# A Mamba/HGRN2/PEER block: the first head prepared in the first mixer, a one-hot on another engine, a deeper pipeline in the last head, one gate stage moved, one product for four

## The chip, the cores and the metric

The program runs on one core of a Trainium2 chip. Times are microseconds on the device, from the start of the execution to its end. A time of a kernel is the median of its runs; the profile is one execution more, with its own time.

## What is computed

A block of a sequence model over 1024 tokens of width 1024, all in float32:

```python
hn = rmsnorm(x, ln_mix_w)
z, xbc, dt_raw, q, f, i, g = split(hn @ w_in)
y_ssd = ssd_mixer(z, xbc, dt_raw, ...)      # 16 heads in 4 groups
y_hg = hgrn2_mixer(q, f, i, g, lb, ...)     # 8 heads of 128
h = x + concat(y_ssd, y_hg) @ w_out
h = h + peer_ffn(rmsnorm(h))                # 8 heads, the best 16 of 128 x 128 experts
return rmsnorm(h)
```

In a chunk of the SSD mixer the decays are exp of differences of cumulative sums of `a`; the HGRN2 mixer has the gate `f = lb + (1 - lb) sigmoid(f_raw)`, its logarithm summed within a chunk, and products of q and k weighted by exp of such sums. For each token and head `peer_ffn` takes rows of two tables of 16384 x 1024: `gelu(x . u) * gate * v`, summed.

## The kernel before

It is written by hand for each engine, with semaphores; each engine runs its queue in order. Five blocks follow one another, with a barrier between them: `input_norm`, `ssd`, `hgrn`, `mix_out`, `peer`. A block of tokens ("chunk") has P = 128; there are NB = 8 chunks, in two halves of HC = 4.

`ssd` runs over four groups of four heads. For each chunk TensorE makes a first stage: `ps_cb`, three transposes and `ps_rows`, the cumulative sums spread over rows, as four products with `awide` (GpSimd's `a` times ones) as weights (L424). Behind them it makes two pieces of the next group's projection (`piece`; in the last group `head_piece`, the first HGRN2 head's q, f and v/g pieces, L396 and L399, which ScalarE copies into unused columns of `Y`, L472). Then comes the second stage, `ps_y` and `ps_state` (from L438), for which VectorE must have made `att` (L625); VectorE's state update waits for it (L631). VectorE and ScalarE prepare the next half (`prepare`, four parts, one per chunk, between `att` and the state update). In the last four chunks of the last group there is nothing more to prepare.

`hgrn` starts with a zero fill of the table `sel` in HBM, issued by ScalarE (L857), then copies the pieces from `Y` (L797), and prepares half 0 of head 0 in four parts (`prepare`): sigmoid, affine map, logarithm, a scan, seven levels of differences, exponentials, and products with k and q (the last are L931 and L932). TensorE's first stage of a chunk is L774 to L777 (seven levels, one product k q, a transpose of `ke`), then come pieces of the next head (L755, L759), then the second stage, `ps_state` and two products into `ps_o` (L785 to L788). VectorE masks the levels (L949, L951) and sums them to `att` (L955), prepares a part, and updates the state (L962) and the output (L965). Seven heads run in a loop, the eighth apart: it has no next head's pieces. ScalarE squares its output (L851), and there the rows of `Y` (L845).

`mix_out` is the output projection and the routing of the first four blocks of tokens, whose experts are not gathered but computed densely: a table of gates `sel` says what gate each expert has for each of these tokens. The first block's entries are scattered by GpSimd.

`peer` first makes the entries of `MB` = 3 blocks: 96 groups of four tokens. VectorE compares a row of numbers with the first keys (`hot_a`, one wide compare, L1908) and with the second keys times the gate (`hot_b`, four instructions, L1912), TensorE multiplies them (L1719), ScalarE copies the two halves of the result into stages (`place_out`, L1793 and L1796), two groups in rotation. SyncE stores a stage when 16 groups are in it (L1622); the fourth stage is `ur`, the ring of u rows. At groups 24 and 60 VectorE routes a unit in between. Then SyncE loads the first u columns (L1627), ScalarE loads gates (L1823), and 256 slots run. In each TensorE makes eight products of 128x512 for one expert column (`ps_d`, L1738) or for one output tile (`ps_o`, L1751); VectorE multiplies the hidden values with the gates (L1924), and for the other four blocks makes two dots with gathered u rows (L1937) and adds two gathered v rows (L1948). GpSimd issues the gathers (L1648, L1655), five rows deep in each ring:

```python
pool.wait_ge(sel_out[3], sel_stores(3))
for r in range(RING):
    u_row(r)
for r in range(RING):
    v_row(r)
```

## Time and profile before

| what | us |
|---|---|
| median of three runs (lowest to highest) | 3722.78 (3721.39 to 3723.29) |
| the profiled execution | 3722.1 |
| its span, first to last instruction | 3720.4 |
| TensorE busy | 3466.2 (93%) |
| VectorE busy | 2888.3 (78%) |
| ScalarE busy | 992.5 (27%) |
| GpSimd busy | 1430.4 (38%) |
| end of the first mixer, and of the second | 532.4, 1161.6 |
| start of `peer`, and of its slots | 1610.2, 1810.5 |

A busy share is an average over the five blocks, in which different engines wait; it says nothing of one boundary. So the profile is read in stretches of time: who is idle in one, and what ended the idle time. PE is TensorE, PEld its weight loads, DVE VectorE, ACT ScalarE, POOL GpSimd, SP SyncE; a `q` behind a name is the engine's issuing of DMAs. A 128x512 float32 product appears as two passes.

### The profile page before, as it was taken

The numbers are of one execution on the slowest core, as the hardware profiler recorded it, in microseconds if no ns is written. First come the engines' busy times: TensorE is split into PE (matmuls) and PEld (weight loads), VectorE is DVE, ScalarE is ACT, GpSimd is POOL, SyncE is SP. The second block draws the span as 40 slices with busy tenths as digits, with TensorE's granted clock in tenths as the row PEclk, the third lists the DMA queues.
The fourth block names the chain that finished last, engine by engine and source line by source line (L and its number), as shares of the span: only waits on it lengthen the run. The fifth ranks groups of instructions, "written<-read, shape, count | busy, mean of one in ns | idle before, by whom it ended". The sixth has DMA issues, their size and how long they took to land.

```text
span 3720.4 us, 40149 instructions
## 1 busy us (share of the span) xinstructions
PE 3466.2 (93%) x11785; PEld 2008.2 (54%) x11785; DVE 2888.3 (78%) x6816; ACT 992.5 (27%) x2460; POOL 1430.4 (38%) x1232
## 2 busy tenths in 40 slices
PE   7999969999997998756799999999999999999997
PEld 4666656777774565445444444444444444444443
DVE  2466657777774299989588888888988889888997
ACT  3333334444442222133211121112112121111211
POOL 1000000000001077500356666565666666665664
PEclk9999989999996999979999999999999999999999
...
GB/s 109 35 29 34 0 92 45 23 23 33 24 11 132 49 57 77 45 58 137 320 384 383 397 383 378 382 392 378 360 375 393 388 387 377 382 391 383 383 388 301
DMA packets 313936, 829.65 MB, mean 223 GB/s; under 512 B 41504, under 2 KB 145056, under 8 KB 305056
## 3 DMA queue, kind: packets, MB, share of 16 engines
...
q8 instruction: 69, 1.13, 0.1%
q14 instruction: 107, 0.88, 0.1%
...
## 4 chain that ended last, share of the span: by engine, by line
PE 49%; DVE 4%; DMA 2%; issue 1%; POOL 0%; ACT 0%; SPq 0%; ACTq 0%; DVEq 0%; POOLq 0%
PE peer_ps_o L1751 23%; PE peer_ps_d L1738 21%; PE peer_ps_q L1680 2%; DVE peer_mt L1912 2%; PE peer_ps_o L1719 1%; DMA peer_vr<-in_v_rows,peer_index 1%; DVE peer_mt L1908 1%; DMA peer_ur<-in_u_rows,peer_index 0%; DMA sel<-peer_ur 0%; DVE Y L1948 0%; PE peer_ps_s L1690 0%; POOL peer_vr L1655 0%; DVE Y L1965 0%; POOL peer_ur L1648 0%; DVE peer_ur L1937 0%
## 5 line engine op out<-in xcount | busy, mean ns | idle before, releaser
L1648 POOL DMA_INDIRECT peer_ur<-in_u_rows,peer_index x512 | 563.3, 1100 | 766.9 <-DVE peer_ur L1937 403.6
L1948 DVE SCALAR_TENSOR_TENSOR Y<-peer_vr,peer_hid,Y 128x1024 f32<-128x1024 f32 x512 | 657.2, 1284 | 83.3 <-DMA peer_vr<-in_v_rows,peer_index 79.7
L1655 POOL DMA_INDIRECT peer_vr<-in_v_rows,peer_index x512 | 597.7, 1167 | 196.8 <-issue 151.3
L1937 DVE SCALAR_TENSOR_TENSOR peer_ur<-peer_ur,Y 128x1024 f32<-128x1024 f32 x512 | 627.8, 1226 | 44.3 <-DMA peer_ur<-in_u_rows,peer_index 43.4
L1738 PE MATMUL peer_ps_d<-hnT,route_ut 128*128 128x512 f32 x1376 | 600.2, 593 | 11.2 <-DMA route_ut<-in_u_cols 11.2
L1751 PE MATMUL peer_ps_o<-peer_va,Y 128*128 128x512 f32 x1024 | 444.3, 594 | 10.2 <-DVE Y L1924 10.2
L1738 PEld LDWEIGHTS peer_ps_d<-hnT,route_ut 128*128 128x128 f32 x1376 | 261.8, 190 | 340.2 <-issue 328.6
L1751 PE MATMUL peer_ps_o<-hnT,Y 128*128 128x512 f32 x1024 | 442.1, 592 | 0.0
L1751 PEld LDWEIGHTS peer_ps_o<-peer_va,Y 128*128 128x128 f32 x1024 | 195.0, 191 | 250.9 <-issue 236.6
L1751 PEld LDWEIGHTS peer_ps_o<-hnT,Y 128*128 128x128 f32 x1024 | 193.5, 190 | 238.2 <-issue 238.2
L1738 PE MATMUL peer_ps_d<-hnT,peer_ut 128*128 128x512 f32 x672 | 295.3, 592 | 0.0
L1406 POOL DMA_INDIRECT sel<-route_ut,mo_sel_index x128 | 209.1, 1634 | 174.6 <-DVE route_ut L1094 113.5
L1811 ACT ACTIVATE peer_act_out<-peer_dots 128x2 f32<-128x2 f32 x256 | 51.3, 200 | 815.5 <-DVE peer_ur L1937 777.1
L1804 ACT ACTIVATE Y<-peer_ps_d 128x512 f32<-128x512 f32 x128 | 76.4, 597 | 694.4 <-PE peer_ps_d L1738 676.5
L1392 POOL IOTA mo_count_u<- 128x128 uint32 x1 | 0.2, 239 | 628.9 <-POOLq L659 628.9
L379 PE MATMUL ssd_ps_piece<-hnT,w_group 128*128 128x512 f32 x512 | 228.0, 599 | 6.9 <-ACT ssd_raw L463 5.1
L1250 PE MATMUL mo_ps_h<-mo_w,mo_yT 128*128 128x512 f32 x512 | 227.2, 602 | 1.1 <-DVE Y L1461 1.1
L1738 PEld LDWEIGHTS peer_ps_d<-hnT,peer_ut 128*128 128x128 f32 x672 | 127.4, 190 | 159.3 <-issue 159.3
L361 POOL TENSOR_TENSOR ssd_awide<-ssd_a,ones 128x512 f32<-128x512 f32 x32 | 33.7, 1053 | 451.1 <-PE ssd_ps_rows L424 404.0
L759 PE MATMUL hg_ps_piece<-hg_w,hnT 128*128 128x256 f32 x896 | 198.0, 379 | 0.0
L755 PE MATMUL hg_ps_piece<-hnT,hg_w 128*128 128x512 f32 x448 | 198.0, 595 | 0.0
L759 PEld LDWEIGHTS hg_ps_piece<-hg_w,hnT 128*128 128x128 f32 x896 | 168.1, 190 | 21.7
...
## 6 DMA issues: line engine op xcount, KB each, us to landing
...
```

The costliest lines, as they stand in the source:

```text
L379: mm = nc.tensor.matmul(bank, w[:, k, i * P:(i + 1) * P], hnT[:, half, k, :], start=(k == 0), stop=(k == KT - 1))
L755: mm = nc.tensor.matmul(bank, w[:, kt, p * P:(p + 1) * P], hnT[:, half, kt, :], start=(kt == 0), stop=(kt == KT - 1))
L759: mm = nc.tensor.matmul(bank[:, 0:2 * P], hnT[:, half, kt, cols(p - 2)], w[:, kt, 2 * P:4 * P], start=(kt == 0), stop=(kt == KT - 1))
L1250: mm = nc.tensor.matmul(ps_h[:, half, :], yT[:, k, :], w[:, k, half * 512:(half + 1) * 512], start=(k == 0), stop=(k == MT - 1))
L1406: pool.indirect_dma_start(sel.rearrange("a i q two (t o) -> (a i q two t) o", o=1), bass.IndirectOffsetOnAxis(ap=sel_index[:, h, k:k + 1], ...
L1648: pool.indirect_dma_start(ur[:, r % RING, :], None, u_rows, bass.IndirectOffsetOnAxis(ap=index[:, r // TOPK % 4, r % TOPK:r % TOPK + 1], a ...
L1655: pool.indirect_dma_start(vr[:, r % RING, :], None, v_rows, bass.IndirectOffsetOnAxis(ap=index[:, r // TOPK % 4, r % TOPK:r % TOPK + 1], a ...
L1738: mm = nc.tensor.matmul(ps_d[:, e % 2, :], ut[e % UT][:, k, :], xT[:, k, :], start=(k == 0), stop=(k == KT - 1))
L1751: mm = nc.tensor.matmul(ps_o[:, o % OB, :], ht(e, tb), v_tile(e, half), start=(j == 0), stop=(j == GE - 1))
L1804: nc.scalar.activation(ht(e), ps_d[:, e % 2, :], ACT.Gelu).then_inc(gelu_done, 1)
L1937: nc.vector.scalar_tensor_tensor(out=ur[:, s, :], in0=ur[:, s, :], scalar=1.0, in1=Y[:, b, D:MIX], op0=ALU.mult, op1=ALU.mult, accum_out=d ...
L1948: nc.vector.scalar_tensor_tensor(out=hb, in0=vr[:, s, :], scalar=hid[:, c:c + 1], in1=hb, op0=ALU.mult, op1=ALU.add).then_inc(comb_done, 1)
```

## The change

Five edits.

1. `ps_rows` is one product of 128x512: GpSimd multiplies `a` with the triangle, and ones are the weights.
2. A class `Heads` holds the buffers and semaphores of the HGRN2 heads, half by half; those of half 0 lie in the first mixer's weight buffer `w_group`, the heads' weights in its `raw` buffer (`hw`). The four parts of head 0, half 0 are made in the last four chunks of `ssd`, where `prepare` stands in the other groups. The second head's weights are loaded there too. `hgrn` copies only half 1's pieces before its heads.
3. In the last head TensorE makes the first stage of chunk c + 1 ahead of the second stage of chunk c, with second buffers for the odd chunks; VectorE's `attend` of c + 1 stands ahead of its `advance` of c, but behind it at the end of the first half. ScalarE's squares of `Y` stand behind its square of the output.
4. The fourth `hot_b` of a group is made by ScalarE, in two activations: the absolute difference, then `relu(gate - gate * difference)`.
5. The fourth stage lies in `vr`, so that u rows are gathered without a wait for the stores, and SyncE's loads of the first three u columns stand ahead of its last two stores.

```diff
@@ ssd @@
+            sp.wait_ge(raw_used, past(GROUPS * 2))
+            for i, part in enumerate(HG_PARTS):
+                sp.dma_start(H.w[:, :, part], w_hg[1, :, :, part]).then_inc(H.w_in[i], 16)
...
-                                            C["ones"][:].unsqueeze(1).to_broadcast([P, HPG, P]),
+                                            C["tri"][:].unsqueeze(1).to_broadcast([P, HPG, P]),
...
-                    for r in range(HPG):
-                        mm = nc.tensor.matmul(ps_rows[:, r, :], awide[:, r, :], C["tri"][:], start=True, stop=True)
-                    mm.then_inc(stage_a, 1)
+                    nc.tensor.matmul(ps_rows[:].rearrange("p r l -> p (r l)"), C["ones"][:],
+                                     awide[:].rearrange("p r l -> p (r l)"), start=True, stop=True).then_inc(stage_a, 1)
...
+                    elif c % HC < 3:
+                        if c % HC == 0:
+                            act.wait_ge(H.lb_diff, past(1))
+                            nc.scalar.activation(H.lb[:], H.lb[:], ACT.Sigmoid).then_inc(H.lb_ready, 1)
...
+                        heads_act(nc, act, H, 0, 0, c % HC, first_raw(Y, 0)[0:3])
...
+                    else:
+                        if c % HC == 0:
+                            dve.wait_ge(H.lb_in, 16)
...
+                            dve.wait_ge(H.lb_ready, past(2))
+                            dve.wait_ge(piece_out, past(GROUPS * 2 * SSD_PIECES + HG_PIECES))
+                        heads_dve(nc, dve, head_prep, H, 0, 0, c % HC, C["reset"][:, 0:HALF], first_raw(Y, 0)[3])
@@ hgrn, TensorE @@
             def body(u, last):
+                if last:
+                    pe.wait_ge(piece_out, past(HEADS * 2 * HG_PIECES))
+                    first_stage(u, 0, 1)
                 for c in range(NB):
...
                     if not last:
+                        first_stage(u, c, 0)
                         for p in HEAD_PARTS[c % HC]:
...
+                    elif c + 1 < NB:
+                        first_stage(u, c + 1, 1)
+                    second_stage(u, c, 1 if last else 0)
@@ hgrn, VectorE @@
+                    if last and c + 1 < NB and c != HC - 1:
+                        attend(u, c + 1, 1)
+                    advance(u, c)
+                    if last and c == HC - 1:
+                        attend(u, c + 1, 1)
@@ peer @@
-        stage = [wide(va[:]), wide(vb), Y[:, 0:4, D:MIX], ur[:, 0:4, :]]
+        stage = [wide(va[:]), wide(vb), Y[:, 0:4, D:MIX], vr[:, 0:4, :]]
...
+                if x == HALVES - 2:
+                    sp.wait_ge(pick_turned, MB)
+                    for e in range(UT):
+                        sp.dma_start(ut[e], u_cols[e]).then_inc(u_in[e], 16)
...
-            pool.wait_ge(sel_out[3], sel_stores(3))
             for r in range(RING):
                 u_row(r)
+            pool.wait_ge(sel_out[3], sel_stores(3))
             for r in range(RING):
                 v_row(r)
...
+                pe.wait_ge(last_ready, j + 1)
                 need(pe, staged, 2 * (j - 1))
...
+            def hot_last(j):
+                b, t = j // (P // 4), j % (P // 4) * 4 + 3
+                act.wait_ge(pick_out, b + 1)
+                need(act, sel_made, j - 1)
+                to = hot_b[j % 2][:, 3, :]
+                nc.scalar.activation(to, R.count[:], ACT.Abs, scale=-1.0,
+                                     bias=pickedT[:, b % 2, 1, t:t + 1]).then_inc(last_apart, 1)
+                act.wait_ge(last_apart, j + 1)
+                nc.scalar.activation(to, to, ACT.Relu, scale=pickedT[:, b % 2, 3, t:t + 1],
+                                     bias=pickedT[:, b % 2, 2, t:t + 1]).then_inc(last_ready, 1)
...
                 place_out(j, 0)
+                if j + 2 < M_GROUPS:
+                    hot_last(j + 2)
                 place_out(j, 1)
...
-                for q in range(4):
+                for q in range(3):
```

ScalarE in the last four chunks of the first mixer, before (`ssd_natural` begins a chunk, `Y<-ssd_ps_piece` is the copy of a piece):

```order
L502 ACTIVATE ssd_natural<-ssd_ps_turn 128x384
L504 ACTIVATE ssd_dec<-ssd_dec 128x512
L472 ACTIVATE Y<-ssd_ps_piece 128x512
L502 ACTIVATE ssd_natural<-ssd_ps_turn 128x384
L504 ACTIVATE ssd_dec<-ssd_dec 128x512
L472 ACTIVATE Y<-ssd_ps_piece 128x512
```

The same place now, up to the second chunk's `dec`:

```order
L604 ACTIVATE Y<-ssd_ps_piece 128x512
L646 ACT_TABLE_LOAD
L646 ACTIVATE head_lb<-head_lb 128x8
L648 ACTIVATE head_oml<-head_lb 128x8
L322 ACTIVATE w_group<-Y 128x512
L323 ACT_TABLE_LOAD
L323 ACTIVATE w_group<-Y 128x512
L324 ACTIVATE head_gs<-Y 128x512
L326 ACT_TABLE_LOAD
L326 ACTIVATE w_group<-w_group 128x512
L634 ACTIVATE ssd_natural<-ssd_ps_turn 128x384
L636 ACT_TABLE_LOAD
```

The first part of the head stands between the copy of a piece and the next chunk, with three table loads, and the next `dec` has a fourth ahead of it.

TensorE at the start of the last head, before and now:

```order
L774 MATMUL hg_ps_att<-hg_W 128x64 x7
L776 MATMUL hg_ps_att<-hg_q,hg_k 128x128
L777 MATMUL hg_ps_turn<-ident,hg_ke 128x128
L785 MATMUL hg_ps_state<-hg_v,hg_ken 128x128
L786 MATMUL hg_ps_o<-hg_state,hg_qs 128x128
L788 MATMUL hg_ps_o<-hg_v,hg_att 128x128
```

```order
L915 MATMUL hg_ps_att<-w_group 128x64 x7
L916 MATMUL hg_ps_att<-w_group 128x128
L917 MATMUL hg_ps_turn<-ident,w_group 128x128
L915 MATMUL hg_ps_piece<-w_group 128x64 x7
L916 MATMUL hg_ps_piece<-w_group 128x128
L917 MATMUL hg_ps_turn<-ident,w_group 128x128
L927 MATMUL hg_ps_state<-head_v,hg_ken 128x128
L928 MATMUL hg_ps_o<-hg_state,w_group 128x128
L930 MATMUL hg_ps_o<-head_v,hg_att 128x128
```

A second first stage stands ahead of the second stage; it writes to the bank of the pieces.

## Rows read from the trace of the kernel before

**Rows 1.** Busy time by stretch; behind the engines: granted clock, DMA share, GB/s.

```profile
533.00:567.00 34.00, 1.67 (x8) 1.71 (x9) 15.04 (x38) 17.37 (x32) 0.14 (x1) 0.51 0.93 309
...
1134.00:1160.00 26.00, 18.21 (x74) 15.91 (x75) 13.72 (x40) 10.52 (x25) 0.00 (x0) 0.50 0.00 1
...
1792.00:1890.00 98.00, 79.09 (x216) 41.01 (x217) 50.56 (x96) 15.48 (x40) 44.31 (x40) 0.92 1.01 386
1890.00:3720.00 1830.00, 1802.73 (x4498) 844.04 (x4496) 1603.58 (x2891) 344.93 (x1039) 1116.71 (x984) 1.00 0.98 379
```

**Rows 2.** Timeline, a late chunk of `ssd`: start, us, engine, line, what.

```profile
499.77 1.06 PE L424 MATMUL ssd_ps_rows<-tri,ssd_awide 128*128 128x128 f32 x8
500.67 7.03 PE L396 MATMUL ssd_ps_piece<-hnT,Y 128*128 128x512 f32 x16
509.49 0.43 DVE L631 TENSOR_TENSOR ssd_state<-ssd_state,ssd_decay_all 128x256 f32<-128x256 f32 x1 [3.61 <-PE ssd_ps_state L442]
```

**Rows 3.** Timeline, the boundary of the two mixers.

```profile
533.17 10.14 ACTq L857 DMA_DIRECT2D sel<-hg_zero  x2
...
544.41 1.32 ACT L797 ACTIVATE hg_raw_vg<-Y 128x256 f32<-128x256 f32 x4
...
565.33 3.22 PE L774 MATMUL hg_ps_att<-hg_W 128*128 128x64 f32 x14 [35.66 <-DVE hg_qs L932]
...
569.08 2.56 PE L755 MATMUL hg_ps_piece<-hnT,hg_w 128*128 128x512 f32 x3
```

**Rows 4.** Timeline, TensorE and ScalarE in chunk 5 of the last head.

```profile
1137.42 3.09 PE L774 MATMUL hg_ps_att<-hg_W 128*128 128x64 f32 x14
...
1140.83 0.42 PE L777 MATMUL hg_ps_turn<-ident,hg_ke 128*128 128x128 f32 x1
...
1144.49 0.79 PE L788 MATMUL hg_ps_o<-hg_v,hg_att 128*128 128x128 f32 x2 [1.59 <-DVE hg_att L955]
1145.08 3.09 PE L774 MATMUL hg_ps_att<-hg_W 128*128 128x64 f32 x14
...
1142.64 1.06 ACT L845 ACTIVATE hg_raw_f<-Y 128x1024 f32<-128x1024 f32 x1
```

**Rows 5.** Timeline, groups of the gate table; the last row follows an interruption.

```profile
1744.54 0.68 DVE L1908 TENSOR_TENSOR peer_mt<-route_count,peer_pickedT 128x512 f32<-128x512 f32 x1
...
1745.14 1.11 DVE L1912 TENSOR_SCALAR peer_mt<-route_count,peer_pickedT 128x128 f32<-128x128 f32 x4
1745.89 0.38 ACT L1796 ACTIVATE peer_va<-peer_ps_o 128x256 f32<-128x256 f32 x1 [0.97 <-PE peer_ps_o L1719]
1746.17 0.68 DVE L1908 TENSOR_TENSOR peer_mt<-route_count,peer_pickedT 128x512 f32<-128x512 f32 x1
1746.17 0.38 ACT L1796 ACTIVATE hnT<-peer_ps_o 128x256 f32<-128x256 f32 x1
...
1746.35 1.13 PE L1719 MATMUL peer_ps_o<-peer_mt 128*128 128x128 f32 x8 [0.50 <-issue]
...
1665.35 3.75 PE L1719 MATMUL peer_ps_o<-peer_mt 128*128 128x128 f32 x16 [9.69 <-issue]
```

**Rows 6.** Groups by line: two copies of ScalarE; busy us, mean ns.

```profile
L1319 ACT ACTIVATE mo_yT<-mo_ps_y,mo_mw 128x128 f32<-128x128 f32 x128 | 34.6, 382 | 58.1 <-PE mo_ps_y L1232 58.1
...
L836 ACT ACTIVATE hg_ken<-hg_ps_turn 128x128 f32<-128x128 f32 x64 | 17.2, 269 | 34.7 <-PE hg_ps_turn L777 34.5
```

**Rows 7.** Timeline, the start of the expert loop.

```profile
1797.72 8.75 SPq L1627 DMA_DIRECT2D route_ut<-in_u_cols  x2
...
1809.81 1.01 POOL L1648 DMA_INDIRECT peer_ur<-in_u_rows,peer_index  x1 [242.54 <-DMA sel<-peer_ur]
1810.49 15.61 PE L1738 MATMUL peer_ps_d<-hnT,route_ut 128*128 128x512 f32 x32 [11.15 <-DMA route_ut<-in_u_cols]
...
1820.96 1.22 DVE L1937 SCALAR_TENSOR_TENSOR peer_ur<-peer_ur,Y 128x1024 f32<-128x1024 f32 x1 [30.78 <-DMA peer_ur<-in_u_rows,peer_index]
...
1888.90 3.64 PE L1751 MATMUL peer_ps_o<-peer_va,Y 128*128 128x512 f32 x4 [7.59 <-DVE Y L1924]
```

393 lines of the change are left out of this document (226 added, 167 removed).

## The prediction

> **What bounds the kernel now.** I read the profile by stages, since the share of busy time over the whole span (TensorE 93%) hides four places where TensorE is not the limit. The table of stretches comes first. From 1890 us to the end TensorE is busy 1802.7 of 1830 us [rows 1]: nothing in the change touches these products, so this part can only start earlier. The gains must come from what lies before it.
>
> The first place is the boundary between the two mixers: from 533 to 567 us TensorE works 1.67 us of 34 while VectorE and ScalarE prepare the first half of the first head (15.0 and 17.4 us busy) [rows 1]. TensorE's first product comes at 565.33 after 35.66 us of idling, its first projection piece at 569.08 [rows 3]. The second is the last head, which has no next head's pieces to fill TensorE: one chunk follows another every 7.66 us (1137.42 to 1145.08) at a granted clock of 0.50 [rows 1, 4]. The third is the making of the gate table: VectorE issues without a gap, a group every 1.63 us (1744.54 to 1746.17), and TensorE's 1.13 us and ScalarE's two copies fit in [rows 5]. The fourth is the start of the expert loop: TensorE waits 11.15 us for the first u columns, GpSimd's first u row waits for the last gate store until 1809.81, and TensorE then waits another 7.59 us for VectorE at 1888.90 [rows 7], in a stretch whose DMA share is 1.01 [rows 1].
>
> **One product for the sums.** Before, four 128-column products with their weights stream per chunk; after, one of 512 columns. Start to start the old group takes 500.67 - 499.77 = 0.90 us; two passes of the 512-column kind take 2 x 7.03/16 = 0.88 us [rows 2]. The same columns are streamed. 32 chunks x 0.03 = 1 us. Bounds: 3 us gained if the last result is there sooner, 2 us lost if it is there later. I take **-1**.
>
> **First head in the first mixer.** Removed from the boundary: all that stands between the ScalarE's zero-fill issue and 565 us. What is late next? TensorE may do the first chunk's products at once, but the next head's first piece waits until five of the six copies of half 1 are out, and these stand on ScalarE behind the issue of the zero fill, 10.14 us from 533.17 [rows 3]. That issue ends at 543.3; two wide copies lead to 544.4, and three of the four narrow ones (1.32 together) to 545.4 [rows 3]. The piece started at 569.08, so -23.7 us, if the first mixer ended when it does now.
>
> It doesn't. The last four chunks get the preparation: about 14 us of VectorE work (the 15.04 us of the boundary without the clearing) [rows 1]. VectorE waits 3.61 us in such a chunk for TensorE [rows 2], so there is room for 14.4 us, but unevenly: the four parts are, by count of instructions, 1.4, 4.0, 5.4 and 3.3 us. Worse, in the first of them VectorE stands in its queue behind a semaphore of ScalarE, whose own queue first has the copy of a piece that TensorE ends at 507.7 [rows 2], and then a table load and three small activations. Queued behind that wait are the state update, the output of the chunk and the next chunk's decay, and TensorE's next second stage waits for them. Worked through chunk by chunk: 1 us late after the first, 3 us by the third, 4.8 us at the end. Then about 1 us since TensorE has idled in between and takes up the piece at the low clock. -23.7 + 4.8 + 1 = **-18**. Bounds: -22 if the overhang is 1 us, -12 if it is 10 (a table load for every change of function in all four chunks). The load of the second head's weights moves into the first mixer behind a wait that is long satisfied, on a SyncE queue with nothing behind it: nothing.
>
> **Last head two chunks deep.** TensorE now does the products of chunk c+1 ahead of the second stage of chunk c, and VectorE's masks of c+1 lie beside it. At the low clock TensorE's own work in a chunk is 3.83 us (1137.42 to the end of the transpose at 1141.25) and three products at 0.59 us (1144.49 to 1145.08) = 5.6 us [rows 4], against some 4.0 of VectorE (13.7 us busy in 26, at 7.66 a chunk) [rows 1]. TensorE becomes the bound: 7.66 - 5.6 = 2.1 us x 4 chunks = 8.2 us. In the chunks before, VectorE is the bound in both, since it prepares half 1. Given back: the two squares of Y per chunk now stand behind the square of the output, so after the last chunk ScalarE has 2 x 1.2 us left (1.06 us each and its read) [rows 4]. -8.2 + 2.4 = **-6**. Bounds -3 (chunk 4 refills the pipeline, since TensorE's second stage of chunk 3 stands behind its wait for half 1's weights) and -12 (the rival on the clock).
>
> **One of four one-hots by ScalarE.** VectorE: 0.60 us for the wide compare and 4 x 0.257 (1745.14 to 1746.17) [rows 5]; one gone makes 1.37 us. ScalarE gets two activations of 128x128 between its two copies, the second waiting for the first. No row has them. From below: a copy of that size without a pointer operand, 0.269 us; from above one with a per-partition scale, 0.382 [rows 6], and 0.11 more for the second operand of the last, 0.49. Its group is then 0.28 (start to start of the copies) + 0.27 + 0.27 + 0.38 = 1.20 at least, and 0.28 + 0.38 + 0.49 + 0.38 = 1.53 at most without any overlap [rows 5, 6]. TensorE of group j+2 now waits for these too: copies and one-hot (1.45) plus its own 1.13 plus some 0.15 of handing over, for two groups, is 1.37 a group. So three engines meet at nearly the same period; with some jitter I take 1.42. 96 x (1.63 - 1.42) = 20 us, less 2 us: after each interruption TensorE runs two groups in 3.75 us at the low clock, 1.88 each [rows 5], whatever VectorE does. **-18**. Bounds: 1.50 gives -10, 1.37 gives -23.
>
> The Trainium skill ("ScalarE: Activation LUTs", What ACT_TABLE_LOAD costs) prices a pointer operand at 93 ns and says that neighbours overlap by as much. The 0.113 us between the two rows of [rows 6] agrees roughly. By it the two would be 0.39 and 0.48 us and ScalarE's group, as an estimate, 1.37 us: this part would be -23, and the total 3664 us.
>
> **Gate pieces in the v ring, u columns early.** On SyncE the three u column loads go ahead of the last two stores; their 8.75 us of issue [rows 7] lies in the 16 x 1.42 = 23 us in which the last batch is made. TensorE, which ended its query at 1799.3, starts 11.15 us sooner [rows 7]. The five u rows (2.6 MB) leave ahead of the stores too; with 1.5 MB of columns that is 4.1 MB less for a stretch that moves 386 GB/s [rows 1], 10.6 us. So VectorE's rows, which first landed at 1820.96 [rows 7], and the v rows behind them move by about the same as TensorE, and the wait at 1888.90 stays at some 7.6 us. The v rows still wait for the last store, but no longer behind the issue of five u rows of 1.0 us and more each [rows 7]. **-10.5**. Bounds: -14, and 0 if the wait there grows by all of it.
>
> **The rivals.**
> (a) The start of the loop is given back. DMA is full there, and the chain goes to VectorE's products of slot 7. If v rows, not u rows, set VectorE's pace, the wait at 1888.90 grows from 7.6 to 18 us and the fourth part is worth nothing: 3669 + 10 = 3679. For it: the DMA share of 1.01. Against: 4.1 MB really leave that stretch.
> (b) The last head rises to 2.4 GHz. Its granted clock is 0.50 while TensorE is busy 18.2 of 26 us [rows 1]; the making of the table holds the full clock at 1.13 of 1.63 us [rows 5], the same share with denser products. After, TensorE has no gap at the low clock. At the high one its chunk is 2.8 us, VectorE's 4.0 binds, and 4 x (7.66 - 4.0) - 2.4 = 12 instead of 6: 3663. The Trainium skill ("TensorE: Matmul & The Clock Gate", Part 1) has sustained activity release the throttle, which speaks for this rival; the row of 26 us shows no rise, but its work had gaps.
> (c) ScalarE sets the table's period at 1.60 us or more: the dependent pair doesn't overlap at all and the handing over costs 0.1 more. Then the fourth edit gives 2 us: 3685.
> (d) Slower than before: the two-deep rotation of the table collapses. If TensorE's group j+1 can't run beside ScalarE's group j, since its one-hot comes too late in ScalarE's queue, the period is 1.13 + 1.53 + 0.1 = 2.76 us: +108 us against 35.5 gained elsewhere, 3795. It decides from 1.63 + 35.5/96 = 2.00 us on. Against it: the one-hot of j+2 stands ahead of the second copy of j.
> (e) The edits don't do what they say: the first mixer's end grows by all that the boundary loses, and the rest cancels: 3722.
>
> **How the numbers follow.** The profiled execution took 3722.1 us with a span of 3720.4, 0.7 us below the median of 3722.78. 3722.1 - 1 - 18 - 6 - 18 - 10.5 = 3668.6, and 3669 on the scale of the median. Chances: this sum 0.50, (a) 0.17, (b) 0.18, (c) 0.11, (d) 0.02, (e) 0.02. The range takes in (a) and (b) and most of the bounds of the two parts of 18: 3650 to 3688. A measurement of this kernel can tell 0.2%, 7.4 us, from no change. Faster: (a), (b), (c) and the forecast, 0.96; same 0.02; slower 0.02.
>
> **What would show it.** The first piece of the second mixer starts about 18 us sooner, 12 us after the zero fill's issue began, and the first mixer ends some 5 us later than now. The last head's chunks 5 to 7 follow every 5.6 us with the clock at 0.50, or every 4.0 with it at 1.00. The table's groups follow every 1.37 to 1.45 us, with ScalarE nearly without idle time. The first u column product follows the query at once, and TensorE's wait for VectorE in the first group of slots is still 6 to 9 us. Wrong would be: a period of the table over 1.5, a wait of 18 us there, or TensorE waiting in the first mixer's last chunks for over 10 us together.

## The result, and the profile after

| kernel | median us | lowest to highest | ratio, 95% interval |
|---|---|---|---|
| before | 3722.09 | 3720.26 to 3723.29 | |
| after | 3664.64 | 3663.56 to 3669.48 | 0.9849 [0.9833, 0.9864] |

The change takes 57.5 us off; 3669 was forecast, with a range of 3650 to 3688. The profiled execution after took 3663.56 us (span 3661.8), 58.5 less than the one before.

A sum that comes out can hide wrong terms, so the two traces are first laid side by side. Each row below is the time between two landmarks that both programs have: the starts of the named instructions, and for the last head the end of its last product.

| stretch | before | after | difference |
|---|---|---|---|
| start to first copy of a chunk (`natural`) in the first mixer | 120.63 | 120.34 | -0.29 |
| from there to the copy of the 29th chunk, 28 chunks | 372.14 | 371.18 | -0.96 |
| last four chunks, to the last write of `Y` | 39.23 | 42.59 | +3.36 |
| to the first piece of the second mixer | 37.08 | 11.99 | -25.09 |
| to its first second stage | 7.98 | 9.19 | +1.21 |
| to the end of the last head's last product | 583.56 | 572.58 | -10.98 |
| to `mix_out`'s first product | 9.69 | 9.84 | +0.15 |
| to the table's first product | 444.35 | 446.32 | +1.97 |
| to the query behind the table | 177.50 | 157.47 | -20.03 |
| to the first u column's product | 18.33 | 7.01 | -11.32 |
| to the last product of the loop | 1889.61 | 1893.05 | +3.44 |

The stretches of Rows 1, now (the table of stretches, same columns; the bounds are moved with the program):

```profile
535.00:569.00 34.00, 26.87 (x103) 17.27 (x104) 14.80 (x45) 13.86 (x25) 0.26 (x1) 0.77 0.74 248
1105.00:1128.00 23.00, 18.21 (x98) 17.35 (x98) 14.70 (x46) 8.68 (x23) 0.00 (x0) 0.65 0.00 0
1741.00:1832.00 91.00, 81.01 (x221) 41.74 (x222) 52.27 (x97) 16.06 (x45) 40.54 (x37) 0.96 1.01 381
1832.00:3661.00 1829.00, 1801.09 (x4492) 843.04 (x4490) 1600.28 (x2888) 344.31 (x1036) 1117.12 (x983) 1.00 0.98 379
```

At the boundary TensorE now works 26.87 of 34 us instead of 1.67 [rows 1]. From the first product of the last head's chunk 4 to the head's end it takes 22.4 us (1105.46 to 1127.87), where it took 31.1 (1129.53 to 1160.62). The busy time of 18.21 us is by chance the one of [rows 1]: there it is 74 products, here 98, part of them at the higher clock. The long last stretch is what it was.

**The boundary.** Timeline after, which answers to [rows 3]:

```profile
535.29 8.58 ACTq L1011 DMA_DIRECT2D sel<-hg_zero  x2
535.69 3.22 PE L915 MATMUL hg_ps_att<-w_group 128*128 128x64 f32 x14 [4.86 <-SPq L109]
...
545.03 1.32 ACT L953 ACTIVATE hg_raw_vg<-Y 128x256 f32<-128x256 f32 x4
546.10 9.36 PE L894 MATMUL hg_ps_piece<-hnT,hw 128*128 128x512 f32 x16 [6.44 <-ACT hg_raw_vg L953]
...
555.29 0.39 PE L927 MATMUL hg_ps_state<-head_v,hg_ken 128*128 128x128 f32 x2
```

TensorE begins at 535.69 instead of 565.33. Its first piece is then held for 6.44 us, until the fifth of ScalarE's six copies (the third narrow one) is out at 546.04, and these copies stand behind 8.58 us of issuing the zero fill. The issue is the bound that the prediction named.

**The end of the first mixer.** TensorE's waits in its last four chunks:

```profile
507.76 0.67 PE L570 MATMUL ssd_ps_y<-ssd_state,ssd_xc 128*128 128x256 f32 x2 [1.35 <-DVE ssd_att L766]
528.84 0.67 PE L570 MATMUL ssd_ps_y<-ssd_state,ssd_xc 128*128 128x256 f32 x2 [0.70 <-DVE ssd_att L766]
```

Two waits, 2.05 us together, both for VectorE's `att`, each behind a chunk in which the preparation had more work than room. With the preparation back at the boundary (below) neither is there.

**The last head.** TensorE in chunks 4 to 7, and then the table of stretches (its column of granted clock stands behind the five engines), which answer to [rows 4]:

```profile
1105.46 3.25 PE L915 MATMUL hg_ps_att<-head_W 128*128 128x64 f32 x14 [9.76 <-DVE head_qs L385]
...
1110.53 3.09 PE L915 MATMUL hg_ps_piece<-head_W 128*128 128x64 f32 x14
...
1115.44 2.53 PE L915 MATMUL hg_ps_att<-head_W 128*128 128x64 f32 x14
...
1119.47 1.68 PE L915 MATMUL hg_ps_piece<-head_W 128*128 128x64 f32 x14
...
1122.74 0.46 PE L927 MATMUL hg_ps_state<-head_v,hg_ken 128*128 128x128 f32 x2 [1.22 <-ACT hg_junk L985]
...
1126.26 0.76 PE L927 MATMUL hg_ps_state<-head_v,hg_ken 128*128 128x128 f32 x2 [2.61 <-ACT hg_junk L985]
```

```profile
1105.50:1117.00 11.50, 11.50 (x54) 11.50 (x55) 6.06 (x20) 0.92 (x4) 0.00 (x0) 0.50 0.00 1
1117.00:1124.00 7.00, 5.06 (x40) 4.46 (x39) 6.54 (x23) 4.56 (x12) 0.00 (x0) 0.98 0.00 0
1124.00:1130.00 6.00, 1.62 (x6) 1.35 (x6) 2.08 (x5) 5.15 (x14) 0.00 (x0) 0.50 0.00 0
```

First stages follow one another after 5.1, 4.9 and 4.0 us and the last two second stages after 3.5, where a chunk took 7.66. TensorE works without any gap at 1.2 GHz until 1117, then has 2.4 GHz for 7 us, then 1.2 again.

The row of 9.76 us is the end of the first half: TensorE is ahead by then and waits for VectorE, which prepares half 1. Counted from the second mixer's first second stage, chunk 4 begins after 550.17 us (552.47 before), so 2.3 of the 11.0 us that this stretch gains lie ahead of chunk 4 and 8.7 behind it. Of the 8.7, the three steps from chunk 4 to chunk 7 gain 9.2 (14.0 us against 23.2), and from chunk 7's first stage to the end it takes 0.5 us more (8.4 against 7.9).

**The table of gates.** VectorE and ScalarE around one group, which answer to [rows 5] (L1903 is the absolute difference, L1906 the `relu`, L1922 and L1919 the copies):

```profile
1735.26 0.69 DVE L2038 TENSOR_TENSOR peer_mt<-route_count,peer_pickedT 128x512 f32<-128x512 f32 x1
...
1735.46 0.39 ACT L1903 ACTIVATE peer_mt<-route_count,peer_pickedT 128x128 f32<-128x128 f32 x1
...
1735.89 0.49 ACT L1906 ACTIVATE peer_mt<-peer_mt,peer_pickedT 128x128 f32<-128x128 f32 x1
1736.29 0.37 ACT L1922 ACTIVATE peer_vr<-peer_ps_o 128x256 f32<-128x256 f32 x1
1736.61 0.38 ACT L1919 ACTIVATE Y<-peer_ps_o 128x256 f32<-128x256 f32 x1
1736.68 0.69 DVE L2038 TENSOR_TENSOR peer_mt<-route_count,peer_pickedT 128x512 f32<-128x512 f32 x1
...
1736.89 0.40 ACT L1903 ACTIVATE peer_mt<-route_count,peer_pickedT 128x128 f32<-128x128 f32 x1
```

Both VectorE (1735.26 to 1736.68) and ScalarE (1735.46 to 1736.89) are at it without a gap. Groups start 1.42 and 1.38 us apart in turn; before it was 1.63 [rows 5]. Of the 95 steps from group to group, 86 are at this pace (121.2 us, 140.2 before) and gain 19.0 us; the other nine, the two interruptions and the slow groups at the start and behind them, go from 35.4 to 34.4 us and gain 1.0.

**The start of the expert loop**, which answers to [rows 7]; L2054 is VectorE's product of hidden values and gates:

```profile
1748.51 13.90 PE L1852 MATMUL peer_ps_d<-hnT,route_ut 128*128 128x512 f32 x32
...
1767.98 0.69 DVE L2054 TENSOR_TENSOR Y<-Y,peer_mt 128x512 f32<-128x512 f32 x1 [26.18 <-issue]
...
1817.91 0.68 DVE L2054 TENSOR_TENSOR Y<-Y,peer_mt 128x512 f32<-128x512 f32 x1
...
1818.65 1.12 PE L1865 MATMUL peer_ps_o<-peer_va,Y 128*128 128x512 f32 x2 [1.04 <-DVE Y L2054]
...
1826.94 0.68 DVE L2054 TENSOR_TENSOR Y<-Y,peer_mt 128x512 f32<-128x512 f32 x1
...
1827.68 23.16 PE L1865 MATMUL peer_ps_o<-peer_va,Y 128*128 128x512 f32 x50 [7.91 <-DVE Y L2054]
```

The first u product follows the query without a gap (11.15 us of waiting before), and the waits at the first output products are 1.04 and 7.91 us against 7.59.

### The profile page after: what moved, and what is told of

Same layout as the page of the kernel before. It is cut to its first block, busy times and chain, and to the rows that moved or that the text cites. A ratio compares the mean times of both kernels' runs of the same rounds, so it can differ in the third digit from the quotient of the medians.

```text
span 3661.8 us, 40046 instructions
## 1 busy us (share of the span) xinstructions
PE 3457.3 (94%) x11593; PEld 1984.5 (54%) x11593; DVE 2862.0 (78%) x6720; ACT 1059.2 (29%) x2649; POOL 1436.1 (39%) x1232
## 4 chain that ended last, share of the span: by engine, by line
PE 48%; issue 4%; DVE 2%; DMA 1%; POOL 0%; ACT 0%; ACTq 0%; DVEq 0%; POOLq 0%
PE peer_ps_o L1865 24%; PE peer_ps_d L1852 22%; PE peer_ps_q L1793 2%; DMA peer_vr<-in_v_rows,peer_index 1%; DVE peer_mt L2038 0%; DVE peer_mt L2042 0%; DVE Y L2078 0%; DMA peer_ur<-in_u_rows,peer_index 0%; PE peer_ps_s L1803 0%; DVE Y L2095 0%; POOL peer_ur L1761 0%; POOL peer_vr L1768 0%; DVE peer_ur L2067 0%; PE peer_ps_o L1833 0%; DVE route_hit L1197 0%
## 5 line engine op out<-in xcount | busy, mean ns | idle before, releaser
L1865 PE MATMUL peer_ps_o<-peer_va,Y 128*128 128x512 f32 x1024 | 446.1, 596 | 12.7 <-DVE Y L2054 12.7
L494 POOL TENSOR_TENSOR ssd_awide<-ssd_a,tri 128x512 f32<-128x512 f32 x32 | 34.5, 1077 | 451.4 <-PE ssd_ps_rows L556 404.3
L894 PE MATMUL hg_ps_piece<-hnT,hw 128*128 128x512 f32 x448 | 199.2, 598 | 6.4 <-ACT hg_raw_vg L953 6.4
L898 PE MATMUL hg_ps_piece<-hw,hnT 128*128 128x256 f32 x896 | 198.0, 379 | 0.0
L898 PEld LDWEIGHTS hg_ps_piece<-hw,hnT 128*128 128x128 f32 x896 | 168.1, 190 | 21.7
```

The source lines that it names most:

```text
L894: mm = nc.tensor.matmul(bank, w[:, kt, p * P:(p + 1) * P], hnT[:, half, kt, :], start=(kt == 0), stop=(kt == KT - 1))
L898: mm = nc.tensor.matmul(bank[:, 0:2 * P], hnT[:, half, kt, cols(p - 2)], w[:, kt, 2 * P:4 * P], start=(kt == 0), stop=(kt == KT - 1))
L1865: mm = nc.tensor.matmul(ps_o[:, o % OB, :], ht(e, tb), v_tile(e, half), start=(j == 0), stop=(j == GE - 1))
```

## The experiments

Twelve kernels. Five undo one edit each, two undo half of one, four lighten or move what may bound a place, and one moves a load together with two of those improvements. In the diffs the lines with a minus are the changed kernel's. The time "before" was 3724.0, 3723.4 and 3723.5 us in the three series, so that ratios are the better measure between them. It matters: by the medians the five undoings cost 21.0, 13.3, 17.7, 10.5 and 5.4 us in the order below, by the ratios 17.5, 10.4, 14.1, 8.2 and 3.7, and each ratio has an interval of some 6 us to either side. The starting point of the first chunk scatters from 119.4 to 124.0 us between the profiled executions; where a few us matter, stretches between landmarks are compared and not whole times.

### Each edit undone

**The preparation back at the boundary.**

```diff
@@ ssd @@
-                        heads_act(nc, act, H, 0, 0, c % HC, first_raw(Y, 0)[0:3])
...
-                        heads_dve(nc, dve, head_prep, H, 0, 0, c % HC, C["reset"][:, 0:HALF], first_raw(Y, 0)[3])
@@ hgrn @@
+            for part in range(3):
+                heads_act(nc, act, H, 0, 0, part, first_raw(Y, 0)[0:3])
...
+            for part in range(4):
+                heads_dve(nc, dve, prep, H, 0, 0, part, C["reset"][:, 0:HALF], first_raw(Y, 0)[3])
```

> The changed kernel with the first head's half 0 prepared behind the barrier between the mixers again (its raw pieces read straight from Y, second head's weights still loaded early). Theory: everything else is additive, and the second edit is worth what the last head's start showed, 21.8 us less 1.2 of the first edit: 3664.6 + 20.6 = 3685 us, the first mixer's last VectorE instruction 2 us sooner than in the changed kernel, TensorE's first product of the second mixer some 30 us behind it. Rival: part of the gain came from the weights and the shorter zero-fill issue (8.58 us against 10.14), which stay: 3681 us or less.

Measured: 3685.62 us, ratio 0.9896 [0.9879, 0.9912]. The first mixer's last four chunks take 39.11 us (42.59 in the changed kernel, 39.23 before), without any wait of TensorE; from the last write of `Y` to the first second stage it is 43.2 us (21.2). Together 18.5 us, and 1.5 more between there and the last head's end, where the higher clock ended with the chunk before the last (0.50 from 1138.0 on) and the last part took 9.8 us instead of 8.4. The theory holds to 2 us at its place; the whole time can't tell 3685 from the rival's 3681. What is missing from the 20.6 us is mostly the issue of the zero fill, which took 8.59 us here and 10.14 in the trace of before [rows 3], as the rival had it. The early load of the weights isn't shown to be the cause: it stays in the kernel with four sums too, and there the issue took 9.88.

**The last head one chunk deep.**

```diff
@@ hgrn, TensorE @@
...
-                    elif c + 1 < NB:
-                        first_stage(u, c + 1, 1)
-                    second_stage(u, c, 1 if last else 0)
+                    second_stage(u, c, 0)
...
```

ScalarE's and VectorE's queues go back to one chunk alike.

> The changed kernel with its last head one chunk deep again (one bank, one att, one ken), the squares of Y still behind the square of the output. Theory: the depth alone is worth the 9.2 us that the span from the last head's start to the output projection lost: 3673 to 3674 us, chunks 5 to 7 every 7.7 us at a granted clock of 0.50. Rival: the place of the squares is a part of it (before, they stood in front of the square of the output, and TensorE's next second stage waited for that one): then chunks follow faster than 7.66 us, about 6.6, and the kernel takes about 3669 us.

Measured: 3677.92 us, ratio 0.9877 [0.9861, 0.9894]. From the first second stage to the last head's end it takes 582.20 us, 9.6 more than with the depth. The profiled executions are 14.9 us apart, since this one's first chunk began 3.3 us later and its expert loop took 1.2 us more; such differences lie between all the kernels here. Its chunks and the table of stretches:

```profile
1125.44 3.09 PE L915 MATMUL hg_ps_att<-head_W 128*128 128x64 f32 x14
...
1133.07 3.09 PE L915 MATMUL hg_ps_att<-head_W 128*128 128x64 f32 x14
```

```profile
1110.00:1142.00 32.00, 22.84 (x92) 19.88 (x92) 14.86 (x46) 9.86 (x27) 0.00 (x0) 0.50 0.00 0
```

7.63 us a chunk at a granted clock of 0.50: the rival falls, since with the squares behind the square of the output chunks follow no faster. The head as a whole is 1.4 us shorter than before (582.20 against 583.56), 1.1 of it ahead of chunk 4, where no square of `Y` stands; which part of the change gives that is open. Here TensorE has a gap in every chunk and stays at 1.2 GHz to the end of the head; in the changed kernel it had none before the clock rose.

**The fourth one-hot on VectorE.**

```diff
-                for q in range(3):
+                for q in range(4):
...
-                if j + 2 < M_GROUPS:
-                    hot_last(j + 2)
...
```

> The changed kernel with all four second one-hots on VectorE. Theory: the table's period is VectorE's sum, 1.63 us against about 1.40 here, over 96 groups 22 us less about 2 at the start: 3664.6 + 20 = 3685 us. Rival: the period stays under 1.55 since other parts of the change (the stage in the v ring, the loads ahead of the stores) made the table faster: under 3678 us.

Measured: 3682.37 us, ratio 0.9887 [0.9871, 0.9904]. The stretch of the table is 177.50 us, to the hundredth that of before, with groups 1.63 us apart:

```profile
1749.97 0.68 DVE L2033 TENSOR_TENSOR peer_mt<-route_count,peer_pickedT 128x512 f32<-128x512 f32 x1
...
1751.60 0.68 DVE L2033 TENSOR_TENSOR peer_mt<-route_count,peer_pickedT 128x512 f32<-128x512 f32 x1
```

So the whole 20 us of this stretch are the one-hot's. The whole time (17.7 us more by the medians, 14.1 by the ratios) would hardly tell the theory's 3685 from the rival's 3678; the stretch does.

**The fifth edit undone.**

```diff
@@ SyncE @@
-                if x == HALVES - 2:
-                    sp.wait_ge(pick_turned, MB)
-                    for e in range(UT):
-                        sp.dma_start(ut[e], u_cols[e]).then_inc(u_in[e], 16)
...
+            sp.wait_ge(pick_turned, MB)
+            for e in range(UT):
+                sp.dma_start(ut[e], u_cols[e]).then_inc(u_in[e], 16)
@@ stage, GpSimd @@
-        stage = [wide(va[:]), wide(vb), Y[:, 0:4, D:MIX], vr[:, 0:4, :]]
+        stage = [wide(va[:]), wide(vb), Y[:, 0:4, D:MIX], ur[:, 0:4, :]]
...
+            pool.wait_ge(sel_out[3], sel_stores(3))
             for r in range(RING):
                 u_row(r)
-            pool.wait_ge(sel_out[3], sel_stores(3))
```

> The changed kernel with the fourth stage in the u ring and the u columns behind the last stores, as before the change. Theory: TensorE waits 11 us for the first u column again, and the wait of 7.9 us for VectorE (1.0 + 7.9 + 3.8 in three waits) goes back to 7.6 + 2.6: 11.3 + 0.9 of low clock - 2.5 = 9.7 us at most, of which the stage table showed 7.9: 3672.5 to 3674.5 us. Rival: the chain through the rows gives it back, and the kernel stays within 3 us of 3664.6.

Measured: 3675.17 us, ratio 0.9871 [0.9854, 0.9887], 10.5 us above the changed kernel by the medians and 8.2 by the ratios. The first u product comes 18.39 us behind the start of the query, against 7.01, so at that place the edit is worth 11.4 us; behind it there is one wait of 6.33 us at the output products instead of 1.04 and 7.91. The whole is a little above the range expected (3672.5 to 3674.5), and the rival, that the rows give it back, falls.

**Four products for the sums.**

```diff
-                    nc.tensor.matmul(ps_rows[:].rearrange("p r l -> p (r l)"), C["ones"][:],
-                                     awide[:].rearrange("p r l -> p (r l)"), start=True, stop=True).then_inc(stage_a, 1)
+                    for r in range(HPG):
+                        mm = nc.tensor.matmul(ps_rows[:, r, :], awide[:, r, :], C["tri"][:], start=True, stop=True)
+                    mm.then_inc(stage_a, 1)
```

> The changed kernel with four products of 128 columns for the sums again. Theory: 0.03 to 0.04 us for each of 32 chunks, 1.2 us later at the end of the first mixer, 3666 us. Rival: no difference, since VectorE's decay waits on something else: the end of the first mixer stays within 0.3 us. One measurement can tell the two only in the profile's chunk periods.

Measured: 3670.07 us, ratio 0.9859 [0.9844, 0.9874]; a single us can't be read from that. The 28 chunks can: 372.13 us here, 372.14 before, 371.18 in the changed kernel. The edit gives 0.034 us a chunk. One thing more goes with it, which the expectation didn't have: from the last write of `Y` to the first piece it is 1.3 us longer here, and the zero fill's issue takes 9.88 us. In the two kernels with four products it took 9.88 and 10.14 us, in the ten with one product that issue it from ScalarE 8.56 to 8.59. By this undoing the edit is worth 2.3 us in the two places. Why the issue should depend on it is open.

### What bounds the boundary

**The zero fill issued by SyncE.**

```diff
@@ hgrn @@
-            act.wait_ge(zero_ready, 1)
+            sp.wait_ge(zero_ready, 1)
             for part in range(P // SELB):
                 pairs = slice(part * KEYS // 4, (part + 1) * KEYS // 4)
-                act.dma_start(sel[:, pairs, 0:P // SELB].rearrange("a i q two t -> a i (q two t)"),
+                sp.dma_start(sel[:, pairs, 0:P // SELB].rearrange("a i q two t -> a i (q two t)"),
...
```

> The changed kernel with the zero fill of the gate table issued by SyncE, whose queue has nothing to do there, instead of ScalarE. Theory: the boundary is bound by that issue, behind which the six copies stand. TensorE's 6.44 us of idling ahead of the first piece go, the piece starts about 4 us behind the barrier at 535 instead of 11, and the whole kernel gains 6 us: 3658.5 us. Rival: VectorE or ScalarE's preparation of half 1 is as late, TensorE waits for that in chunk 0 or 1, and the kernel stays within 2 us of 3664.6.

Measured: 3658.46 us, ratio 0.9828 [0.9814, 0.9841], 6.2 us below the changed kernel's median. The two intervals overlap a little, and the profiled execution, the slowest of its five, is only 2.6 us shorter than the changed kernel's, so the stretches decide.

```profile
536.34 8.49 SPq L875 DMA_DIRECT2D sel<-hg_zero  x2
...
540.09 9.27 PE L899 MATMUL hg_ps_piece<-hnT,hw 128*128 128x512 f32 x16
```

The issue takes as long, on a queue that nobody waits for; the piece follows the first stage without a gap. The first second stage starts 6.1 us sooner (549.19 against 555.29), though the first chunk began 0.6 us later: from the last write of `Y` it is 14.5 us instead of 21.2, so 6.7 us are gained here. The last head takes as long as before behind it (572.1 against 572.6). In this execution the table and the loop give 3.3 us back, at places where the kernels scatter by as much. The theory holds.

### What bounds the last head

**The squares of Y spread over eight chunks.**

```diff
-                    if last and half == 1:
-                        for b in (2 * (c % HC), 2 * (c % HC) + 1):
...
+                    if last:
...
+                        nc.scalar.activation(raw_vg[:, 0:HC, :].rearrange("p c x -> p (c x)"), Y[:, c, 0:D], ACT.Square,
+                                             accum_out=ysq[:, c:c + 1]).then_inc(y_squared, 1)
...
```

> The changed kernel with the eight squares of Y one in every chunk of the last head (written to the free half of the v and g pieces), behind the square of the output, in the last chunk ahead of it. Theory: ScalarE's pair of squares (2.4 us) sets the pace of chunks 6 and 7 and the tail: TensorE's waits of 1.22 and 2.61 us for the square of the output go, and 2.4 us behind the last one: 3 to 5 us sooner, 3660.5. Rival: in the first four chunks ScalarE also prepares half 1, and there TensorE waits 2.96 and 2.18 us for the square of the output already: a square more in each costs 1.2 us there, and the sum is 0 to -1: 3664 us.

Measured: 3662.20 us, ratio 0.9837 [0.9823, 0.985], between the two forecasts (3660.5 and 3664), which it can't tell apart. Half of the theory falls. TensorE's waits in chunks 6 and 7 stay:

```profile
1121.63 0.28 ACT L985 ACTIVATE hg_junk<-hg_ps_o 128x128 f32<-128x128 f32 x1 [2.16 <-DVE Y L1065]
...
1122.26 0.46 PE L927 MATMUL hg_ps_state<-head_v,hg_ken 128*128 128x128 f32 x2 [0.93 <-ACT hg_junk L985]
...
1125.74 0.46 PE L927 MATMUL hg_ps_state<-head_v,hg_ken 128*128 128x128 f32 x2 [2.58 <-ACT hg_junk L985]
```

ScalarE now stands idle 2.16 us ahead of that square, waiting for VectorE's output; the releaser that the profile names is the last link only. VectorE is the bound: in the changed kernel it starts the masks of one chunk at 1118.46 and of the next at 1122.00, 3.54 us later, without a gap between. What the spreading gives is the tail: last head's end to `mix_out`'s first product 8.71 us against 9.84. Of the first half the rival was right that it gives nothing, but wrong that it costs: chunk 4 begins at the same distance (550.19 us against 550.17).

### What bounds the table

**Less on ScalarE, less on VectorE.** Both kernels leave part of the one-hots out.

```diff
@@ no_abs @@
-                nc.scalar.activation(to, R.count[:], ACT.Abs, scale=-1.0,
-                                     bias=pickedT[:, b % 2, 1, t:t + 1]).then_inc(last_apart, 1)
-                act.wait_ge(last_apart, j + 1)
-                nc.scalar.activation(to, to, ACT.Relu, scale=pickedT[:, b % 2, 3, t:t + 1],
+                nc.scalar.activation(to, R.count[:], ACT.Relu, scale=pickedT[:, b % 2, 3, t:t + 1],
@@ one_fewer_on_vector @@
-                for q in range(3):
+                for q in range(3 if j < 2 else 2):
```

> The changed kernel without the absolute difference in the one-hot that ScalarE makes (the second activation reads the row of numbers itself, so these gates are wrong). It takes 0.39 us per group from ScalarE and nothing from VectorE. If ScalarE sets the period of 1.40 us, it falls to VectorE's sum of about 1.37 or below; if VectorE sets it, it stays at 1.37 to 1.40 and only ScalarE gets idle time. Either way within 4 us of 3664.6, and the gaps tell which.

> The changed kernel with only two of four second one-hots on VectorE from the third group on (the third keeps old contents, so these gates are wrong). It takes 0.257 us per group from VectorE. If VectorE alone sets the period it falls to TensorE's 1.13 plus a handing over, 1.2 us, and the kernel takes 3645 us; if ScalarE stands at the same limit, the period stays at 1.36 to 1.40 us and the kernel at 3662 us or more.

Measured, one run each: 3668.76 and 3664.31 us; the stretch of the table 157.55 and 155.57 us against 157.47. The same table takes 157.2 to 158.9 us in the nine other kernels that have it unchanged, so 1.5 us can be scatter. Without the absolute difference ScalarE waits, and VectorE goes on as before:

```profile
1735.67 0.39 ACT L1916 ACTIVATE Y<-peer_ps_o 128x256 f32<-128x256 f32 x1 [0.33 <-PE peer_ps_o L1833]
1735.74 0.69 DVE L2035 TENSOR_TENSOR peer_mt<-route_count,peer_pickedT 128x512 f32<-128x512 f32 x1
...
1737.16 0.69 DVE L2035 TENSOR_TENSOR peer_mt<-route_count,peer_pickedT 128x512 f32<-128x512 f32 x1
```

With one less on VectorE it is VectorE that waits, at 1.36 to 1.42 us a group:

```profile
1735.85 0.69 DVE L2038 TENSOR_TENSOR peer_mt<-route_count,peer_pickedT 128x512 f32<-128x512 f32 x1 [0.21 <-PE peer_ps_o L1833]
...
1736.06 0.39 ACT L1903 ACTIVATE peer_mt<-route_count,peer_pickedT 128x128 f32<-128x128 f32 x1
...
1737.21 0.69 DVE L2038 TENSOR_TENSOR peer_mt<-route_count,peer_pickedT 128x512 f32<-128x512 f32 x1 [0.15 <-PE peer_ps_o L1833]
```

The mean period at full pace is 1.409 us in the changed kernel, 1.415 without the absolute difference and 1.402 with one less on VectorE. So both engines stand at the same limit, and relieving one alone gives 0.6 us in the 86 steps; the other 1.3 us of one less on VectorE lie in the two interruptions.

### What bounds the start of the loop

**One half of the fifth edit at a time**: the u columns late again with the stage in the v ring, and the stage in the u ring again with the columns early. The diffs are the two halves of the one above.

> The changed kernel with the u columns issued behind the last stores again, the fourth stage left in the v ring. Theory: TensorE's start needs both only in part: the first column lands 11 us late as before the change, so the whole fifth edit is lost but for what VectorE's earlier u rows save of the wait at the first o products (7.9 us falls towards 0 to 3): between 3668 and 3675 us, 3671. Rival: rows give nothing: 3675, like both parts back together.

> The changed kernel with the u columns ahead of the last two stores, but the fourth stage in the u ring, so that u rows wait for the stores. TensorE starts at once. Theory: VectorE's first products then come some 5 us later (five u rows issued in front of five v rows), and TensorE's wait at the first o products grows from 7.9 by as much: 3669 us. Rival: v rows and gates set VectorE's pace there, not u rows, and nothing is lost: within 2 us of 3664.6; then the stage in the v ring is worth nothing.

Measured: 3667.97 us, ratio 0.9849 [0.9834, 0.9864], and 3669.78, ratio 0.9858 [0.9843, 0.9873]. Against the changed kernel's 0.9849 the first ratio is the same and the second 3.4 us worse, both within their intervals, so whole times settle nothing. Where the loss arises is seen at the products of the loop (those for expert columns and output tiles alone), counted from the start of the query (us against before):

| product of the loop | changed | both back | columns late | stage in u |
|---|---|---|---|---|
| 1st | -11.3 | +0.1 | +0.3 | -11.3 |
| 33rd | -12.4 | +1.2 | +0.2 | 0.0 |
| 129th, first output product | -12.2 | +1.2 | +0.2 | +1.5 |
| 161st, behind the waits | -10.8 | +1.3 | -8.0 | -5.4 |
| 3725th | -10.7 | +1.3 | -8.0 | -5.4 |
| last | -7.9 | +3.5 | -5.5 | -3.2 |

```profile
1772.85 2.08 PE L1803 MATMUL peer_ps_s<-route_wk,route_qs 128*128 128x128 f32 x8 [12.10 <-ACT route_qs L1874]
...
1832.84 17.43 PE L1865 MATMUL peer_ps_o<-peer_va,Y 128*128 128x512 f32 x40 [2.39 <-DVE Y L2054]
```

Those are rows of the kernel with the stage in the u ring. Its early columns gain 11 us and are held up 12.10 us later: ScalarE's copy of the query stands in its queue behind the first pair's activation, which needs two dots of u rows, and these rows left only behind the last store. So the number expected for this kernel (3669) came, and its mechanism didn't: the wait at the first output products fell to 2.39 us instead of growing. With late columns it is as expected. TensorE loses 11 us at the start and gets 8 of them back, since VectorE, fed early with u rows, is nearly ready when the output products come, and the wait there falls to 1.10 us:

```profile
1764.96 15.74 PE L1851 MATMUL peer_ps_d<-hnT,route_ut 128*128 128x512 f32 x32 [11.42 <-DMA route_ut<-in_u_cols]
...
1836.81 13.57 PE L1864 MATMUL peer_ps_o<-peer_va,Y 128*128 128x512 f32 x31 [1.10 <-DVE Y L2053]
```

Against both back, at the last product, the stage in the v ring alone gives 9.1 us, the early columns alone 6.7, both 11.4 in the changed kernel. But that last number scatters: in the eight other kernels that carry the whole edit and leave the v columns where they are, it is 9.2 to 12.4. So the two halves don't add up (15.8 us would be the sum); that the early columns still give anything beside the stage is not shown, neither by these 0.1 to 3.4 us nor by the equal ratios. They stand for each other, since behind the first output products it counts when VectorE's chain of dots began.

**The first v columns loaded later**, together with the two improvements above.

```diff
@@ SyncE @@
-            for i in range(2):
-                sp.wait_ge(sel_out[i], sel_stores(i))
-            sp.dma_start(va[:], v_cols[0, 0]).then_inc(v_in[0], 16)
...
+                    if e == UT + 2:
+                        for i in range(2):
+                            sp.wait_ge(sel_out[i], sel_stores(i))
+                        sp.dma_start(va[:], v_cols[0, 0]).then_inc(v_in[0], 16)
```

> The changed kernel with SyncE's zero fill, the spread squares, and the first load of v columns (2 MB, first needed at the first o product, 65 us later) issued behind the third u column that is reloaded, not ahead of the first. The first two are worth 6.1 and 1.1 us by their own profiles: 3657.4. Theory on the start of the loop: the wait of 7.9 us at the first o products is a matter of bytes, the rows and gates that VectorE needs share the queues with those 2 MB; about 5 us of transfers less ahead of them shorten the wait by 3 to 5 us: 3653. Rival: VectorE's start at 1768 is set by the gate load, which waits for all stores, and what follows by GpSimd's rings: the waits stay within 1 us of 12.7 together, and the kernel at 3657.

Measured: 3658.15 us, ratio 0.9828 [0.9815, 0.9842]: as fast as the zero fill's move alone, though two stretches are shorter. The theory falls. The rival's whole time came (3657), but its waits did not stay: the three in the loop are 14.7 us together, not 12.7.

```profile
1751.49 0.69 DVE L2059 TENSOR_TENSOR Y<-Y,peer_mt 128x512 f32<-128x512 f32 x1 [19.98 <-DMA peer_mt<-sel]
...
1810.18 1.13 PE L1870 MATMUL peer_ps_o<-peer_va,Y 128*128 128x512 f32 x2 [3.29 <-DVE Y L2059]
1819.21 24.62 PE L1870 MATMUL peer_ps_o<-peer_va,Y 128*128 128x512 f32 x50 [7.91 <-DVE Y L2059]
```

VectorE's wait ahead of its first gates product is shorter (19.98 against 26.18 us), but the same 2 MB now meet later rows (one v row is waited for 6.47 us at 1775), and the waits at the output products grow from 8.95 to 11.20 us. The bytes needed by then are the same, which is the likely reason; no run varies them.

The second wait is 7.91 us here, in the changed kernel, with the zero fill moved and with four sums. Between the two products with gates that release TensorE VectorE has 9.03 us of fixed work in the changed kernel (1817.91 to 1826.94) and 9.04 before (1879.13 to 1888.17), a block of routing among it. TensorE has 1.12 us of work from one to the other, and 9.03 - 1.12 = 7.91. Both times VectorE works through this without a wait for a row. Where TensorE's 1.12 us lie in a stretch of the lower clock, the wait is shorter by as much as they are longer (7.28 us without the absolute difference). So once TensorE has caught VectorE at the first of these products, an earlier landing can't shorten the second wait.

## Why the prediction was right, point by point

The four places and what bounds each were named rightly. Three sizes were off, one term came out by luck, and two small losses were not seen.

**The sums, -1.** Measured -0.96 over 28 chunks, and given back by the undoing. Right there. The undoing gives back 1.3 us more at the boundary, by a longer issue of the zero fill; no term had that.

**First head in the first mixer, -18.** The terms were -23.7, +4.8 and +1. They measured -25.1, +3.4 and +1.2: -20.5. The bound behind the boundary (the zero fill's issue, then the copies) was the named one, and moving it gave 6.7 us between the landmarks, which shows it. The overhang was mis-sized by 1.4 us: TensorE waited in two of the four chunks for 2.05 us together, where the working let each lateness reach the end. The other 1.4 us are the issue, 8.58 us instead of the 10.14 that the sum took from [rows 3].

**Last head, -6.** Measured -10.8 with the barrier, and 9.6 by the undoing. This is the part that was furthest off, and it has three steps.

First, the pace. 2.1 us x 4 chunks = 8.2 was forecast for the second half, and it gained 8.7, but not so. A chunk at 1.2 GHz took 4.9 us and not 5.6: three products were counted at 0.59 us, from a row behind a wait, and take 0.43 each in a stream (1110.53 - 1109.25 = 1.28), and the first stage was counted to its modelled end, 3.83 us, where the next product starts after 3.63 (1110.53 to 1114.16 in the timeline). Against that, depth shortens three steps and not four: the last chunk's own way to the end got 0.5 us longer. The two errors nearly cancel.

Second, the first half, put at nothing because VectorE is the bound there in both. It gained 2.3 us, 1.1 of which the one-deep kernel has too. That VectorE is the bound holds (TensorE waits 9.76 us for it ahead of chunk 4), but VectorE got there sooner; which of its waits went isn't shown.

Third, the squares' tail, +2.4. It is nearly absent from the whole (9.84 us to `mix_out`'s first product against 9.69), but the cost is there: ScalarE's next block begins 3.63 us behind the last product instead of 1.85, so 1.8 us were given back. They are hidden by luck, since VectorE's first scaling of `Y`, for which TensorE waits there, took 0.75 us instead of 2.49. Before and after:

```profile
1167.76 2.49 DVE L1417 TENSOR_SCALAR Y<-Y,ysq 128x1024 f32<-128x1024 f32 x1
```

```profile
1136.90 0.75 DVE L1528 TENSOR_SCALAR Y<-Y,ysq 128x1024 f32<-128x1024 f32 x1
```

It took 0.75 us in all thirteen kernels that carry the change, the one-deep one among them, and the instruction is the same; why it took 2.49 before is open. Spreading the squares won 1.1 us of the tail.

The rival on the clock (12) was half true. The clock rose in the middle of the second half, and VectorE at 3.5 to 4.0 us bound the last two chunks, as the rival had it. The Trainium skill ("TensorE: Matmul & The Clock Gate", Part 1) says that the throttled state is the default and that activity releases it. The trace agrees in direction (0.50 to 0.98 behind 11.5 us without a gap), and the one-deep kernel agrees from the other side (0.50 throughout). But the rise is worth little here: with the zero fill moved and with the one-hot back it came 5 us behind chunk 4's first product instead of 12 and lasted 13.6 us instead of 7, and the stretch to the head's end took 572.1 us against 572.6. And three steps of 4.9 us would be 14.7 us, where 14.0 were measured. Most of the gain is the depth's.

**One-hot by ScalarE, -18.** Measured -20.0, at a period of 1.41 us (1.42 and 1.38 in turn) against 1.42 forecast. The row estimates lay between 1.20 and 1.53 for ScalarE's group; it takes 1.40. By the prices of the Trainium skill ("ScalarE: Activation LUTs", What ACT_TABLE_LOAD costs) the two activations were estimated at 0.39 and 0.48 us; the trace has 0.39 and 0.49, and the group is a little longer than the 1.37 us estimated from them. The 2 us taken off for the restarts were right in kind: those groups gain little, as forecast, but 1.0 us and not nothing, so that half of the term was lost (19.0 + 1.0). The other 1 us is the period.

**Fifth edit, -10.5.** Measured -11.3 at the first product and -10.8 behind the waits, so the wait did stay. But the reason given, that rows move by as much as the columns, is only part of it: 7.91 us of the 8.95 are VectorE's fixed work. The edit's worth by the undoing is 11.4 us at the last product, 10.5 by the medians and 8.2 by the ratios. The rows' half of the edit, which the prediction needed only so that the gain should not be given back, holds 9.1 us by itself; the early columns, which it put first, are not shown to add to it.

**What was not forecast.** Near the end, in the same place of a later group, TensorE waits again for VectorE's gates product:

```profile
3481.41 19.13 PE L1865 MATMUL peer_ps_o<-peer_va,Y 128*128 128x512 f32 x40 [3.76 <-DVE Y L2054]
```

```profile
3482.50:3486.00 3.50, 3.50 (x6) 1.41 (x5) 3.50 (x5) 0.68 (x3) 1.62 (x2) 0.52 1.02 418
```

Before, the wait was 2.65 us and the clock stayed at 1.00; now it is 3.76, and TensorE goes on at 0.52 for 3.5 us. That costs 2.8 us: 1.1 of wait and 1.7 of clock. Every kernel of this document that carries the change loses something here, 0.7 to 3.8 us. The one with four sums waits 3.32 us and keeps the higher clock, and loses 0.7; the one with the one-hot back waits 2.16 us, less than before, and still has 3.4 us of the lower clock. So no single edit is its cause, and the wait's length alone doesn't decide on the clock. What does is open. "From 1890 us on this part can only start earlier" was too strong. `mix_out` with the start of `peer` took 2.0 us longer, and 0.9 to 2.6 in the other kernels that carry the change (0.9 in both with the squares spread). Some 0.9 us of the 2.0 come between the last product of the start of `peer` and the table's first, where ScalarE makes its first one-hots; with the one-hot back on VectorE this step is absent. The rest wasn't tested.

Of the rivals, (a) the start given back, (c) ScalarE at 1.60, (d) the collapse and (e) the edits without effect didn't come. The sum of the profiled executions: -53.5 forecast, -58.5 measured, of the last head makes -4.8 of the difference, the first head -2.5, the one-hot -2.0, and the two places not forecast +4.9.
